# The last mixer of a fused two-block transformer kernel: its projections read the residual times the norm's weights, and the norm's root is applied behind them

## The reference, cut to what matters

```python
def rmsnorm(t, g, eps=RMS_EPS):
    tf = tf * lax.rsqrt(jnp.mean(tf * tf, axis=-1, keepdims=True) + eps)
    return (tf * g.astype(jnp.float32)).astype(t.dtype)

def diff_attn_mixer(h, w_in, lam_vecs, subln_w, w_out, cos, sin, layer):
    y = h @ w_in
    q, k, v = jnp.split(y, 3, axis=-1)
    q = apply_rope(q.reshape(B, L, DIFF_HEADS, 2, DIFF_HEAD), cos, sin)
    k = apply_rope(k.reshape(B, L, DIFF_HEADS, 2, DIFF_HEAD), cos, sin)
    lam = jnp.exp(jnp.sum(lv[0] * lv[1])) - jnp.exp(jnp.sum(lv[2] * lv[3])) + lam_init
    o = causal_diff_attention(q, k, v, lam)      # softmax(q k / 8), first component minus lam times the second, times v
    o = rmsnorm(o, subln_w, SUBLN_EPS) * (1.0 - lam_init)
    return o.reshape(B, L, D_MODEL).astype(h.dtype) @ w_out

# second_block, for i in range(2):
    hn = rmsnorm(h, g[0])
    m = diff_attn_mixer(hn, ...)                 # i == 1; the other mixer at i == 0
    h = h + rmsnorm(m, g[1])
    f = sq_relu_mlp(rmsnorm(h, g[2]), mlp_w1[i], mlp_w2[i])
    h = h + rmsnorm(f, g[3])
```

## Time and profile before

| what | value |
|---|---|
| median of 3 runs | 1643.39 us |
| span of the profiled execution, first to last instruction | 1634.6 us |
| TensorE busy | 1546.6 us, 95% of the span |
| VectorE busy | 1043.7 us, 64% |
| ScalarE busy | 739.1 us, 45% |
| GpSimd busy | 61.6 us, 4% |
| mean granted TensorE clock | 0.985 of full speed |

### The profile page before, as it was taken

One profiled execution on the slowest core, in us unless ns is written; L12 is line 12 of the kernel. 1 busy time (PEld: TensorE's weight loads), 2 busy tenths in 40 slices (PEclk: granted clock), 3 DMA queues, 4 the chain that ended last, 5 costly groups with the idle time before them and its releaser, 6 DMA issues. The chain is left out here.

```text
span 1634.6 us, 34035 instructions
## 1 busy us (share of the span) xinstructions
PE 1546.6 (95%) x14370; PEld 1489.8 (91%) x14370; DVE 1043.7 (64%) x1583; ACT 739.1 (45%) x1017; POOL 61.6 (4%) x82
## 2 busy tenths in 40 slices
PE   5999999999999898999999999999999998899997
PEld 5999989999999898999988898899999887799997
DVE  7999557997754768444488554555445677565544
ACT  2555444793204734454355020466433445556632
POOL 0122000000010000110000000000000000000000
PEclk9999999999999999999999999999999999999999
DMA  9899644433212446555443000344543332135551
GB/s 371 320 358 346 230 176 181 175 137 118 73 60 104 168 155 228 184 202 174 167 142 107 6 2 2 111 177 176 180 171 113 138 129 79 63 137 186 196 191 52
DMA packets 39202, 256.89 MB, mean 157 GB/s; under 512 B 4259, under 2 KB 5668, under 8 KB 9892
## 3 DMA queue, kind: packets, MB, share of 16 engines
q1 hardware_dynamic: 37492, 251.07, 42.4%
q10 hardware_dynamic: 1584, 3.97, 0.6%
HBM read 251.87 MB, written 3.15 MB: 156 GB/s over the span
## 5 line engine op out<-in xcount | busy, mean ns | idle before, releaser
L473 DVE TENSOR_TENSOR w_lo<-raw,w_hi 128x2048 fp32r<-128x2048 f32 (+2 forms) x203 | 456.4, 2248 | 393.7 <-ACT w_hi L465 393.5
L560 PE MATMUL bank<-x_hi,w_hi 128*128 128x256 f32 (+1 forms) x1832 | 521.9, 285 | 17.7 <-DVE w_lo L473 7.8
L465 ACT ACTIVATE w_hi<-raw 128x2048 fp32r<-128x2048 f32 (+2 forms) x203 | 382.0, 1882 | 300.5 <-PE bank L562 281.3
L562 PE MATMUL bank<-x_hi,w_lo 128*128 128x256 f32 (+1 forms) x1832 | 513.7, 280 | 0.0
L561 PE MATMUL bank<-x_lo,w_hi 128*128 128x256 f32 (+1 forms) x1832 | 513.3, 280 | 0.0
L560 PEld LDWEIGHTS bank<-x_hi,w_hi 128*128 128x128 f32 x1832 | 345.4, 189 | 25.5 <-issue 17.1
L561 PEld LDWEIGHTS bank<-x_lo,w_hi 128*128 128x128 f32 x1832 | 346.1, 189 | 0.9 <-issue 0.7
L562 PEld LDWEIGHTS bank<-x_hi,w_lo 128*128 128x128 f32 x1832 | 345.8, 189 | 0.0
L560 PE MATMUL bank<-mh_hi,w_hi 128*128 128x272 f32 (+1 forms) x512 | 144.3, 282 | 0.0
L562 PE MATMUL bank<-mh_hi,w_lo 128*128 128x272 f32 (+1 forms) x512 | 144.3, 282 | 0.0
L561 PE MATMUL bank<-mh_lo,w_hi 128*128 128x272 f32 (+1 forms) x512 | 144.3, 282 | 0.0
(11 more groups left out here) (582 smaller groups left out, 2545.2 us busy)
## 6 DMA issues: line engine op xcount, KB each, us to landing
raw<-in_stream SPq DMA_DIRECT2D x227, 1024.0 KB, 4.8
raw<-in_stream SPq DMA_DIRECT2D x8, 768.0 KB, 4.1
gate_store<-stage ACTq DMA_DIRECT2D x8, 256.0 KB, 2.0
raw<-in_stream SPq DMA_DIRECT2D x4, 512.0 KB, 3.4
h<-in_h ACTq DMA_DIRECT2D x1, 1088.0 KB, 9.5
zt<-gate_store SPq DMA_DIRECT2D x1, 1024.0 KB, 5.6
gate<-gate_store SPq DMA_DIRECT2D x1, 1024.0 KB, 7.8
out<-h SPq DMA_DIRECT2D x8, 128.0 KB, 1.9
```

The costliest lines, as they stand in the source:

```text
L465: nc.scalar.activation(w_hi[:, s_at % 2, 0:kt], raw[:, r_at % RING, 0:kt], ACT.Copy).then_inc(hi_done, 1)
L473: nc.vector.tensor_tensor(w_lo[:, s_at % 2, 0:kt], raw[:, r_at % RING, 0:kt], w_hi[:, s_at % 2, 0:kt].bitcast(F32), ALU.subtract).then_inc ...
L560: nc.tensor.matmul(out, hi, xh[:, k0 + k, 0:L], start=start, stop=False)
L562: mm = nc.tensor.matmul(out, lo, xh[:, k0 + k, 0:L], start=False, stop=stop)
```

## The change

The projections of the last mixer read `h` times the norm's weight, without the root. Since the root is one factor per token, it can be applied later: to the keys it goes with the sine and cosine tables (`sin_k`, `cos_k`, two products of 272 columns on VectorE), to the values when `value_rows` copies them (a scale column `root_k`, and the copy of 512 columns becomes two of 256), and to the queries as the scale of the exponentials and of their maximum (a column `root_q` in place of the constant 1/8). For the columns TensorE turns the row of roots by five matmuls of one column each (`root_columns`), and VectorE takes them out in four small instructions (`root_columns_out`).

The seam between mlp and attention is written anew. In the mlp the block ends with the root of its own norm. The new block begins with `residual_and_low`, one loop on VectorE that, two tiles apart, multiplies the mlp's output by weight and root, adds it to `h`, and takes `x_lo`. ScalarE makes `x_hi` from `h` as tiles come, with `split_hi` of slab 1 (k0) behind its second tile and the squares of two tiles behind every second. The squares go into `mlp_out`, VectorE adds them up in three steps (1088, 544 and 272 columns), and TensorE makes one sum of them in slot -3, between q0 and k0. The root itself comes in slot -3 on ScalarE, behind `split_hi` of slab 2 (v0), and on VectorE. `split_lo` of slab 1 moves from VectorE to GpSimd, and the exponentials for lambda move from ahead of the slots into slot -2. TensorE's 40 matmuls that nobody reads become 12 in the mlp's block; the 20 at the beginning of the attention stay.

```diff
-UP_BUSY, RECURRENT_BUSY = 28, 50
...
+        class AttentionNorm(LateNorm):
+            def __init__(self, src, L, a_cols):
+                LateNorm.__init__(self, src, L, a_cols)
+                lo_count[0] -= DT
...
+            late = isinstance(then, AttentionNorm)
...
-                        if then:
+                        if then and not late:
...
-                        norm.on_dve(dve, mid)
+                        if late:
+                            norm.root_on_dve(dve)
+                        else:
+                            norm.on_dve(dve, mid)
...
-                        if then:
+                        if late:
+                            keep_busy(hid_hi[:, 0, 0:P], hid_hi[:, 1, 0:T1], SEAM_BUSY)
+                        elif then:
                             keep_busy(hid_hi[:, 0, 0:P], hid_hi[:, 1, 0:T1], GAP_BUSY)
                             for u in range(4):
                                 then.total(pe, u, squares)
...
+            if late:
+                return then, norm, out, kept
+            kept.close()
...
-        before_attention = mlp(S["mlp1_0"], S["mlp2_0"], 0, before_mlp, lambda: Norm(h, T2, g_row(1, 0)), h, T2)
+        before_attention, mlp_norm, mlp_out, mlp_kept = mlp(S["mlp1_0"], S["mlp2_0"], 0, before_mlp, lambda: AttentionNorm(h, T2, g_row(1, 0)), h, T2)
...
-        mid_od = sb("mid_od", [P, DT, T2], c=at_)
...
+        cos_k, sin_k = (sb(n, [P, T2], c=at_) for n in ("cos_k", "sin_k"))
+        root_q, root_k = (sb(n, [P, 4], c=at_) for n in ("root_q", "root_k"))
...
+        ROOT_COLUMNS = [(META, P), (META + P, P), (0, P), (P, P), (2 * P, META)]
...
-                            before_attention.wait_tile(pe, k)
+                            pe.wait_ge(a["x_low"], k + 1)
...
+                def root_columns():
+                    pe.wait_ge(a["root"], 1)
+                    for n, (t0, size) in enumerate(ROOT_COLUMNS):
+                        mm = nc.tensor.matmul(banks[7][0:size, 300 + n:301 + n], stat[0:1, 3, t0:t0 + size], const("ones")[0:1, 0:1], start=True, stop=True)
+                    mm.then_inc(a["root_mm"], 1)
...
+                    if s == -3:
+                        before_attention.one_total(pe, mlp_out)
+                    if s == -1:
+                        root_columns()
...
+            @block.gpsimd
+            def _(pool):
+                sec, g, (r, r_at, s, s_at, landed) = slab(1)
+                pool.wait_ge(hi_done, s + 1)
+                nc.gpsimd.tensor_tensor(w_lo[:, s_at % 2], raw[:, r_at % RING], w_hi[:, s_at % 2].bitcast(F32), ALU.subtract).then_inc(raw_used, 1)
...
+                    if g == 0 and kind == 1 and j == 0:
+                        dve.wait_ge(a["turn_k"], 2)
...
-                    nc.vector.tensor_tensor(by_sin[:, kind, j, 0:n], banks[j][:, 0:n], sin_t[:, cols], ALU.mult).then_inc(a["by_sin"], 1)
-                    nc.vector.tensor_tensor(target(g, kind, j), banks[j][:, 0:n], cos_t[:, cols], ALU.mult).then_inc(dve_took if j else a["half_took"], 1)
+                    cos_x, sin_x = (cos_k, sin_k) if kind else (cos_t, sin_t)
+                    nc.vector.tensor_tensor(by_sin[:, kind, j, 0:n], banks[j][:, 0:n], sin_x[:, cols], ALU.mult).then_inc(a["by_sin"], 1)
+                    nc.vector.tensor_tensor(target(g, kind, j), banks[j][:, 0:n], cos_x[:, cols], ALU.mult).then_inc(dve_took if j else a["half_took"], 1)
...
-                        nc.vector.tensor_scalar(smx[0:C, b, 2:4], smx[0:C, b, 0:2], -scale, None, ALU.mult).then_inc(u_["nmax"], 1)
+                        nc.vector.tensor_scalar(smx[0:C, b, 2:4], smx[0:C, b, 0:2], root_q[0:C, 2 + qt:3 + qt], None, ALU.mult).then_inc(u_["nmax"], 1)
...
-                before_attention.on_dve(dve, mid_od)
-                split_lo(dve, slab(1))
+                def residual_and_low():
+                    for n in range(DT + 4):
+                        if n < DT:
+                            nc.vector.scalar_tensor_tensor(out=mlp_out[:, n], in0=mlp_out[:, n], scalar=mlp_norm.a_cols(n), in1=stat[:, 3],
+                                                           op0=ALU.mult, op1=ALU.mult).then_inc(n_mid, 1)
+                        k = n - 2
+                        if 0 <= k < DT:
+                            dve.wait_ge(n_mid, mlp_norm.mid0 + k + 1)
+                            nc.vector.tensor_tensor(h[:, k], h[:, k], mlp_out[:, k], ALU.add).then_inc(n_lo, 1)
+                        k = n - 4
+                        if k >= 0:
+                            dve.wait_ge(n_hi, before_attention.hi0 + k + 1)
+                            nc.vector.scalar_tensor_tensor(out=x_lo[:, k], in0=h[:, k], scalar=before_attention.a_cols(k), in1=x_hi[:, k].bitcast(F32),
+                                                           op0=ALU.mult, op1=ALU.subtract).then_inc(a["x_low"], 1)
+                def root_of_keys():
+                    inverse_root(dve, n_y, before_attention.q + 1, stat[:, 0], stat[:, 1], stat[:, 2], stat[:, 3], n_ms)
+                    dve.sem_inc(a["root"], 1)
+                    nc.vector.tensor_tensor(sin_k[:], sin_t, stat[:, 3], ALU.mult).then_inc(a["turn_k"], 1)
+                    nc.vector.tensor_tensor(cos_k[:], cos_t, stat[:, 3], ALU.mult).then_inc(a["turn_k"], 1)
+                def root_columns_out():
+                    dve.wait_ge(a["root_mm"], 1)
+                    nc.vector.tensor_scalar(root_q[:, 0:2], banks[7][:, 300:302], scale, None, ALU.mult)
+                    nc.vector.tensor_scalar(root_q[:, 2:4], banks[7][:, 300:302], -scale, None, ALU.mult)
+                    nc.vector.tensor_copy(root_k[:, 0:2], banks[7][:, 302:304])
+                    nc.vector.tensor_copy(root_k[0:META, 2:3], banks[7][0:META, 304:305]).then_inc(a["root_col"], 1)
+                residual_and_low()
+                before_attention.add_squares(dve, mlp_out, 0)
...
-                dve.wait_ge(a["lam_e"], 1)
-                link(dve, "dve", nc.vector.tensor_tensor(lam_s[:, 2:3], lam_s[:, 1:2], lam_s[:, 0:1], ALU.subtract))
-                nc.vector.tensor_scalar(lam_s[:, 3:4], lam_s[:, 2:3], -LAM_INIT, None, ALU.add).then_inc(a["lam_x"], 1)
+                def lam_of_exponentials():
+                    dve.wait_ge(a["lam_e"], 1)
+                    link(dve, "dve", nc.vector.tensor_tensor(lam_s[:, 2:3], lam_s[:, 1:2], lam_s[:, 0:1], ALU.subtract))
+                    nc.vector.tensor_scalar(lam_s[:, 3:4], lam_s[:, 2:3], -LAM_INIT, None, ALU.add).then_inc(a["lam_x"], 1)
...
                     if s == 0:
+                        root_columns_out()
...
+                        if s == -4:
+                            before_attention.add_squares(dve, mlp_out, 1)
+                            before_attention.add_squares(dve, mlp_out, 2)
...
+                        if s == -3:
+                            root_of_keys()
+                        if s == -2:
+                            lam_of_exponentials()
...
+                            if s == -3:
+                                dve.wait_ge(raw_used, slab(1)[2][0] + 1 + RING)
...
-                    nc.scalar.activation(v_at[:, 0:2, 2 * g:2 * g + 2], banks[4][:].rearrange("p (c j n) -> p c j n", c=2, j=2), ACT.Copy).then_inc(a["v_out"], 1)
+                    act.wait_ge(a["root_col"], 1)
+                    for c in range(2):
+                        ins = nc.scalar.activation(v_at[:, c, 2 * g:2 * g + 2], two(banks[4][:, 2 * c * P:2 * (c + 1) * P]), ACT.Copy, scale=root_k[:, c:c + 1])
+                    ins.then_inc(a["v_out"], 1)
...
-                    nc.scalar.activation(v_at[0:META, 2, 2 * g:2 * g + 2], two(banks[5][0:META, 0:2 * P]), ACT.Copy).then_inc(a["v_out"], 1)
+                    nc.scalar.activation(v_at[0:META, 2, 2 * g:2 * g + 2], two(banks[5][0:META, 0:2 * P]), ACT.Copy, scale=root_k[0:META, 2:3]).then_inc(a["v_out"], 1)
...
-                                                   scale=64 ** -0.5, accum_out=smx[0:C, b, 4 + comp:5 + comp])
+                                                   scale=root_q[0:C, qt:qt + 1], accum_out=smx[0:C, b, 4 + comp:5 + comp])
...
-                before_attention.on_act(act, mid_od, lambda: split_hi(act, slab(1)))
-                act.wait_ge(a["lam_x"], 1)
-                nc.scalar.activation(lam_s[:, 0:2], lam_s[:, 0:2], ACT.Exp).then_inc(a["lam_e"], 1)
+                for k in range(DT):
+                    act.wait_ge(n_lo, mlp_norm.lo0 + k + 1)
+                    nc.scalar.activation(x_hi[:, k], h[:, k], ACT.Identity, bias=0.0, scale=before_attention.a_cols(k)).then_inc(n_hi, 1)
+                    if k == 1:
+                        split_hi(act, slab(1))
+                    if k % 2:
+                        before_attention.square(act, k // 2, mlp_out)
...
+                    if s == -3:
+                        before_attention.root_on_act(act)
+                    if s == -2:
+                        act.wait_ge(a["lam_x"], 1)
```

(1 more changed line is left out.)

8 lines of the change are left out of this document (5 added, 3 removed).

## The result

The changed kernel is slower: 1649.97 us against 1646.9 us for the kernel before (medians of the runs that were compared), a ratio of 1.0025 with a 95% interval of 1.0014 to 1.0036. Of 1643.39 us that is +4.1 (2.3 to 5.9); the two medians by themselves lie 3.1 apart. The forecast was -0.5 us, with a range of 1638.0 to 1646.8. The sign was wrong, and +4.1 is more than the slowest of the rivals, B, had (+3.4).

A forecast was written before the change was run, and what follows sets the result against it. TensorE, busy 95% of the span, was taken as the bound. A gain of 6.8 us at k0, less 0.9 (new wait), 1.0 (later work), 3.5 (collision) and 0.9 (clock), left 0.5: 1642.9 us, range 1638.0 to 1646.8.

The forecast's parts named there:

- B: Rival: VectorE stands still for all GpSimd's split, q0's second half at half clock; 3.4 us slower, 1646.8 us; chance 0.17.
- The border: Border between blocks, now between the mlp's root and VectorE's first residual multiplication; priced at 0.82 us.
- the collision: In the residual loop, GpSimd's split of slab 1 makes VectorE stand still 3.9 us, net 3.5.
- the half clock: In q0's second half, a lower clock after TensorE's pause costs 0.9 us, at most 2.8.
- Five matmuls of one column: On TensorE, the matmuls for the scale columns lie beside slots with its own work; cost nothing.
- the delay by lambda's exponentials: At k0's second products on VectorE: about 4 us of delay against 4.7 of cover, hidden by 0.6.
- The new wait ahead of v0: TensorE waits behind k0 for a free bank because the root comes later; about 0.9 us, 0 to 2.3 possible.
- The later work: Values' copies and exponentials with scale columns lengthen two later TensorE waits by 0.5 each; 1.0 us, range 0 to 1.4.
- A: Rival: GpSimd's split runs beside VectorE without collision; 1639.4 us, or 1638.5 with an undisturbed clock; chance 0.21.
- C: Rival: the gain at q1 is eaten at the 3.11 us wait at 1370.23; 1643.9 us; chance 0.05.

The follow-up runs named there:

- e1: The changed kernel with the split of slab 1 back on VectorE, behind the last low part; 1649.64 us, ratio 1.0003 (0.9971 to 1.0034).
- e5: The kernel before with only the split of slab 1 moved to GpSimd; 1647.07 us, ratio 1.0002 (0.9980 to 1.0024).
- e6: The changed kernel rewoven: split on VectorE, squares summed on TensorE, columns between k0 and v0, constant scale from unit 4; 1640.8 us, ratio 0.9977 to before.
- e9: e6 with more unread matmuls in TensorE's pauses ahead of and within q0's first half; 1641.45 us, ratio 0.9979 (0.9948 to 1.0010).
- e10: e6 with the split of slab 1 put back on GpSimd; 1651.22 us, ratio 1.0025 (0.9997 to 1.0054).
- e13: e9 with 24 unread matmuls ahead of v3 and 12 ahead of slot 13's scores; 1639.58 us, ratio 0.9958 (0.9941 to 0.9976).
- e3: The changed kernel with the five one-column matmuls moved from inside v0 to between k0 and v0; 1649.7 us, ratio 1.0006 (0.9978 to 1.0034).
- e8: The changed kernel with the values copied at constant scale in one copy of 512 columns; q1 to v3 takes 76.13 us, in the changed kernel 76.47.

## Why the prediction was wrong

**The seam was right in its mechanism.** The border came at R+1.06 (0.84 said), the collision took 4.0 us of VectorE (3.9 said), the clock fell to half in TensorE's pause, and k0 began at R+18.9 to 19.5 (18.3 to 19.2 said). That k0 fits so well is in part luck: the last low part ended at 1282.99 = R+14.8, 0.6 later than said (14.2, with a net 3.5 for the collision, where 14.81 against e1's 10.88 is 3.9), and the half clock, with 0.9 in the sum, cost 0, 0.4 and 0.6 us. The rule of the Trainium skill on the shared ports ("SBUF — State Buffer", section "Who interferes with whom") fits the three kernels shown here whose split is GpSimd's: steps of 4.43, 4.75 and, within a group, 5.58 for 1.33, beside splits of 4.50 to 5.04. The 4.50 us that the Trainium skill has for such a step on GpSimd ("GPSIMD Engine Reference", section "Elementwise — side-by-side cycle accounting") is what e5's row shows; the other two rows are longer, 4.78 and 5.04. The gain left at k0, 2.1 to 2.7 us, is near the sum's own (6.8 - 3.5 - 0.9 = 2.4).

**The step that failed: "Five matmuls of one column ... lie beside slots in which TensorE has its own work: nothing."** TensorE is the bound, so its own instructions can't lie beside anything; work on the bound costs what it takes unless it falls into a wait. They are ten rows and 1.17 us, all inside v0, and in e6, e9, e10 and e13, where TensorE has no wait left there, k0 to q1 takes 1.22 us more than before. In the changed kernel itself e3 gets only 0.45 of it back, because VectorE then keeps TensorE waiting instead: the delay by lambda's exponentials, which the prediction had as "hidden by 0.6", becomes a wait of 0.57 us in e3. I had named TensorE's share of 95% in the first sentence and then priced its work as if it were another engine's.

**Two terms were too small.** The new wait ahead of v0 was 1.22 and 1.31 us (0.9 said). The later work, 1.0 said with a range to 1.4, measured 2.06 up to the scores of slot 13, in two profiles without a dip of the clock: 1.24 up to v3 and 0.82 behind it. I had seen two waits and blamed the values' copies; e8 puts 0.90 of the first 1.24 on the scales of the exponentials, which I had at 0.1 each in passing, and of their maximum, which I had not counted, and at waits that I had left out because "elsewhere TensorE is ahead".

**The sum, again:** I said -1.5 us at q1 and -0.5 at the end of the attention. The first profile has +0.2 at q1 and +2.3 at the late wait. Of the 1.7 at q1, 1.17 are the columns' rows and 0.3 the wait; 0.5 more pass where TensorE starts again behind the wait and the columns, and k0 itself was 0.3 better than said. The further 1.1 are the later work.

**What I had no term for** is the clock behind v3: the profile of before that I had shows none there, and I took its full clock for the rule. The three profiles of the changed kernel reach the late wait 4.6 us later than the two of the kernel before, on the mean (147.2 and 142.5); the measured 4.1 (2.3 to 5.9) agrees with it. About 2.3 of it are work and waits that the rows show each time, up to 0.6 more come from the clock in q0, and the rest from dips that only some executions have. How that last part splits between the change and chance stays open. So does what lies behind the late wait, whose code no edit touches: from there to the end of the span eleven of the 17 profiles take 233.5 to 235.6 us and six 238.9 to 242.7 (two of the changed kernel's three, neither of the two of before, but e5 as well).

**The rivals.** A, no collision, is refuted by e1, e5 and e10. C, a gain that is lost at the wait ahead of v3, is not borne out: leads over before of 3.13 us (e6) and 4.20 (e9) at q1 are still 2.32 and 3.35 at v3. B had the right sign and the wrong cause: no part of GpSimd's time beyond 4.0 us and no 2.8 us of half clock were needed. The chances went wrong in the same place: B was the only case on the slower side, and the terms with a price of nothing had no range.

## What to carry to other kernels

On the engine that bounds a kernel nothing is free: price each added instruction there at its full time, and look for a wait to put it in. A step taken from a busy VectorE and given to GpSimd, both with two operands in SBUF, can be paid by VectorE nearly at GpSimd's speed; here 2.3 us became 4.0, while GpSimd's row has 5.0. Where a change is worth less than the scatter of an execution, compare distances from an event that it doesn't touch, and take several profiles before a stretch at full clock is believed to be always at full clock.
